# First block's attention taken by pairs of query blocks, with the values as the stationary operand of 256-column matmuls

## The chip, the cores and the metric

The kernel runs on one core of a Trainium2 chip. Its time is the device time of one execution in microseconds; a comparison takes the median of several executions. The profile is one further execution, recorded by the hardware profiler; its times are counted from the start of its span.

## What is computed

Two transformer blocks run one after the other on 2048 tokens of width 1024, all in float32. The change touches only the attention of the first block: 4 heads, queries and keys of 128 + 64 features (the 64 are rotated by position), values of 128, softmax over all 2048 keys with a causal mask by position, then a gate.

```python
def attend(args):
    qn, qr, pq = args
    s = (jnp.einsum('bqhd,bkhd->bhqk', qn, k_nope)
         + jnp.einsum('bqhr,bkr->bhqk', qr, k_rope)).astype(jnp.float32) * scale
    mask = pq[:, None, :, None] >= positions[:, None, None, :]
    p = jax.nn.softmax(jnp.where(mask, s, neg), axis=-1)
    return jnp.einsum('bhqk,bkhd->bqhd', p.astype(v.dtype), v)
...
y_a = mla_branch(...) * jax.nn.silu(gate_a)
```

## The kernel before

The program is written out by hand for each engine; semaphores order the engines against one another. The first block makes keys and values for all tokens, and then goes over four groups of 512 tokens (g = 0 to 3). A group projects its queries and gates, runs the attention of its 4 query blocks of 128 rows, and ends with the output projection (`1out`), which reads the gated attention output from `y_all`, features on the partitions. The second block follows and isn't changed.

Attention goes by units: one query block i and one head h, 16 units in a group, 64 in all. All 2048 keys are taken for every query block. For one unit:

- TensorE makes the scores: 4 tiles of 128 x 512 into four PSUM banks, each with one matmul over 128 features (L1895) and one over the 64 rotated ones (L1899). Neighbouring tiles take the rotated features from the lower and the upper 64 partitions.
- VectorE adds the mask while it moves each tile to the row buffer in `probs` and takes the row's maximum (L1336 to L1343, semaphore `row_max`). `probs` has room for two rows of 2048, which units use in turn.
- ScalarE takes the exponential in place, with the row's sum beside it (L1011, semaphore `probs_made`).
- TensorE turns the row in 16 transposes of 128 x 128 (L1920), four to a bank; ScalarE copies each bank to one of three slots of `prob_t` (L1006); TensorE multiplies the turned probabilities, as stationary operand, with 128 columns of `val` (L1927) and adds up into `o_acc`, which then holds queries on the partitions. `pv_done` counts these groups of four.

On TensorE's queue the scores of unit u stand ahead of the turns and values of unit u - 1. Within a unit the order is: turn 0, turn 1, values 0, turn 2, values 1, turn 3, values 2, values 3 (a turn is 4 transposes, a values step 4 matmuls). After the fourth head VectorE divides by the sums (L1357, L1360, into `o_sb`), TensorE turns the result in 4 transposes (L1906, tile `o_t`), and VectorE multiplies with the gate into `y_all` (L1349).

Six PSUM banks are shared by all tiles in the order of one list: tile number n takes bank n mod 6, and `claim` makes TensorE wait until tile n - 6 has been drained (semaphores `drained`). `tile_ready` counts finished tiles.

Of the kernel before, what the change touches and what calls it, by code (L numbers as in the profile page):

```python
# [7 lines left out]
S = 2048  # L8
P = 128
KC = D // P  # L10
TB = 512
# [51 lines left out]

def mla_units(g):
    return [(BG * g + b, h) for b in range(BG) for h in range(H1)]


def mla_tiles(g):

    units = mla_units(g)  # L70
    for u in range(len(units) + 2):
        if u < len(units):
            yield from [("score", *units[u], c) for c in range(S // TB)]
        if 2 <= u and units[u - 2][1] == H1 - 1:
            yield ("o_t", units[u - 2][0])
        if 1 <= u <= len(units):
            yield from [("prob_t", *units[u - 1], c) for c in range(S // TB)]
# [324 lines left out]
def program(nc, A, out_t):  # L402
# [10 lines left out]
    with ctx:  # L413
# [27 lines left out]
        k_rope = alloc(one, "k_rope", [P, S])  # L441
# [4 lines left out]
        cos = alloc(one, "cos", [P, TB])  # L446
        sin = alloc(one, "sin", [P, TB])
# [4 lines left out]
        mask = alloc(one, "mask", [P, S], bf16)  # L452
# [37 lines left out]
        two.close()  # L490
        mask_i = probs[:, S:S + KC * P].bitcast(i32)
# [96 lines left out]
        o_scaled = sem("o_scaled")  # L588
# [81 lines left out]
        def prev_unit(units, u, g, back):  # L670
            return units[u - back] if u >= back else mla_units(g - 1)[u - back]
# [240 lines left out]
        def _(act):  # L912
# [61 lines left out]
            for g in range(G):  # L974
# [23 lines left out]
                for u in range(len(units) + 1):  # L998
                    if u > 0:
                        i, h = units[u - 1]  # L1000
                        for c in range(S // TB):
                            m = (H1 * BG * g + u - 1) * (S // TB) + c
                            wait_tile(act, "prob_t", i, h, c)
                            if m >= PT_SLOTS:
                                act.wait_ge(pv_done, m - PT_SLOTS + 1)
                            drains(A_(prob_t[:, m % PT_SLOTS, :], bank("prob_t", i, h, c)[:], ACT.Copy), "prob_t", i, h, c)  # L1006
                    if u < len(units):
                        n = H1 * BG * g + u
# [218 lines left out]
        def _(dve):  # L1227
# [45 lines left out]
            for g in range(G):  # L1273
# [3 lines left out]
                step(dve, V.tensor_tensor(k_rope[:, g * TB:(g + 1) * TB], tmp[:, 0, :], tmp[:, 1, :], ALU.add))  # L1277
# [8 lines left out]
            def mask_of(i):  # L1286

                step(dve, V.tensor_scalar(mask[:], pos_k[:], pos_q[:, i:i + 1], MASKED, ALU.is_gt, ALU.mult))

            for g in range(G):  # L1290
# [35 lines left out]
                for u in range(len(units) + 2):  # L1326
                    if u < len(units):
                        i, h = units[u]
                        n = H1 * BG * g + u
                        if h == 0:  # L1330
                            mask_of(i)
                        if n >= 2:
                            wait_tile(dve, "prob_t", *prev_unit(units, u, g, 2), S // TB - 1)
                        for c in range(S // TB):
                            wait_tile(dve, "score", i, h, c)
                            drains(V.tensor_tensor_reduce(out=probs[:, (n % 2) * S + c * TB:(n % 2) * S + (c + 1) * TB],  # L1336
                                                          in0=bank("score", i, h, c)[:], in1=mask[:, c * TB:(c + 1) * TB],
                                                          scale=1.0, scalar=-HUGE, op0=ALU.add, op1=ALU.max,
                                                          accum_out=stat[:, c:c + 1]), "score", i, h, c)
                        for c in range(S // TB):  # L1340
                            wait_drained(dve, "score", i, h, c)
                        step(dve, V.reduce_max(stat[:, 4:5], stat[:, 0:4], AX.X))
                        V.tensor_scalar(stat[:, 8 + n % 2:9 + n % 2], stat[:, 4:5], -QK_DIM ** -0.5, None,  # L1343
                                        ALU.mult).then_inc(row_max, 1)
                    if 2 <= u and units[u - 2][1] == H1 - 1:
# [6 lines left out]
                    if 1 <= u <= len(units) and units[u - 1][1] == H1 - 1:  # L1352
                        i = units[u - 1][0]
# [939 lines left out]
```

## Time and profile before

| | |
|---|---|
| median of 3 executions | 3866.52 us (3864.78 to 3866.83) |
| profiled execution: its time, its span | 3869.51 us, 3867.7 us |
| TensorE busy | 3532.2 us, 91% of the span |
| VectorE, ScalarE, GpSimd busy | 1794.3, 1443.8 and 414.1 us |
| granted TensorE clock, mean | 0.963 of full speed |

The profile lists a float32 matmul as two instructions, since the engine passes over the moving operand twice; a transpose is one. So four matmuls stand as x8 in its rows, and four transposes as x4. A row's own length includes the time in which its last result drains, which overlaps with the next row; what a piece of work costs the engine is the distance from its start to the next row's start. The span contains some 1.8 us less than the time, since launching and ending lie outside it.

### The profile page before, as it was taken

The numbers are of one execution on the slowest core, as the hardware profiler recorded it, in microseconds if no ns is written. First come the engines' busy times: TensorE is split into PE (matmuls) and PEld (weight loads), VectorE is DVE, ScalarE is ACT, GpSimd is POOL, SyncE is SP. The second block draws the span as 40 slices with busy tenths as digits, with TensorE's granted clock in tenths as the row PEclk, the third lists the DMA queues.
The fourth block names the chain that finished last, engine by engine and source line by source line (L and its number), as shares of the span: only waits on it lengthen the run. The fifth ranks groups of instructions, "written<-read, shape, count | busy, mean of one in ns | idle before, by whom it ended". The sixth has DMA issues, their size and how long they took to land.

```text
span 3867.7 us, 40758 instructions
## 1 busy us (share of the span) xinstructions
PE 3532.2 (91%) x15056; PEld 1965.5 (51%) x15056; DVE 1794.3 (46%) x4223; ACT 1443.8 (37%) x2445; POOL 414.1 (11%) x445
## 2 busy tenths in 40 slices
PE   8999999999999999999988989799797898787887
PEld 3445644564466446644555445554445643444653
DVE  3413222331232223223664477825778625879652
ACT  1213312331233113312332355524666515666551
POOL 0001011001200210011111201111011111010100
PEclk9999999999999999989989999899899998998999
DMA  4130013002300230042103211031110031110002
GB/s 172 57 95 23 1 57 117 17 1 65 116 10 1 71 97 1 1 141 82 60 20 100 72 54 47 1 109 66 50 52 1 23 103 53 41 57 1 1 4 85
DMA packets 71893, 205.67 MB, mean 53 GB/s; under 512 B 6376, under 2 KB 7952, under 8 KB 71440
## 3 DMA queue, kind: packets, MB, share of 16 engines
q1 hardware_dynamic: 63360, 187.32, 15.0%
q10 hardware_dynamic: 8336, 15.74, 1.1%
q8 instruction: 121, 1.98, 0.2%
q14 instruction: 76, 0.62, 0.1%
HBM read 185.46 MB, written 17.58 MB: 52 GB/s over the span
## 4 chain that ended last, share of the span: by engine, by line
PE 74%; DVE 11%; ACT 8%; issue 6%; SPq 0%; DMA 0%; POOL 0%; ACTq 0%; DVEq 0%; POOLq 0%
PE bank L1794 38%; PE o_acc L1927 6%; PE bank L1895 6%; PE bank L1899 3%; PE bank L2138 3%; PE bank L2023 3%; PE bank L1920 2%; PE bank L2150 2%; PE o_acc L2164 2%; PE bank L2055 2%; ACT prob_t L1066 2%; ACT pt_last L1066 1%; DVE tmp L1506 1%; ACT prob_t L1006 1%; PE bank L2004 1%
## 5 line engine op out<-in xcount | busy, mean ns | idle before, releaser
L1794 PE MATMUL bank<-group_even,weights 128*128 128x512 f32 x1376 | 603.1, 596 | 17.0 <-DMA weights<-in_w_in_kv 11.7
L1794 PE MATMUL bank<-group_odd,weights 128*128 128x512 f32 x1376 | 607.0, 599 | 6.2 <-ACT tmp L1052 6.2
L1794 PE MATMUL bank<-y_all,weights 128*128 128x512 f32 x1024 | 443.2, 595 | 10.5 <-DVE y_all L1758 6.3
L1794 PEld LDWEIGHTS bank<-group_even,weights 128*128 128x128 f32 x1376 | 261.5, 192 | 337.9 <-issue 337.8
L1794 PEld LDWEIGHTS bank<-group_odd,weights 128*128 128x128 f32 x1376 | 262.5, 193 | 331.2 <-issue 330.9
L1336 DVE CUSTOM_DVE_ANT_0 probs<-bank,mask 128x512 f32<-128x512 f32 x256 | 161.6, 687 | 417.7 <-PE bank L1899 417.7
L1794 PEld LDWEIGHTS bank<-y_all,weights 128*128 128x128 f32 x1024 | 194.5, 191 | 254.4 <-issue 247.1
L1006 ACT ACTIVATE prob_t<-bank 128x512 f32<-128x512 f32 x256 | 145.9, 596 | 430.2 <-PE bank L1920 430.2
L1927 PE MATMUL o_acc<-val,prob_t 128*128 128x128 f32 x2048 | 270.3, 280 | 16.0 <-ACT prob_t L1006 16.0
L1927 PEld LDWEIGHTS o_acc<-val,prob_t 128*128 128x128 f32 x2048 | 247.3, 191 | 31.2 <-ACT prob_t L1006 31.2
L1895 PE MATMUL bank<-k_nope,q_nope 128*128 128x512 f32 x512 | 230.7, 593 | 0.0
L2138 PE MATMUL bank<-kh,qa 64*128 64x512 f32 (+3 forms) x816 | 172.0, 498 | 28.1 <-DVE mx L1716 15.4
L1193 ACT ACTIVATE prob_t<-bank 128x512 f32<-128x512 f32 (+3 forms) x240 | 116.7, 534 | 146.7 <-PE bank L2150 146.4
L2164 PE MATMUL o_acc<-prob_t,v 128*64 128x128 f32 x1680 | 148.0, 284 | 12.2 <-ACT prob_t L1193 8.5
L2164 PEld LDWEIGHTS o_acc<-prob_t,v 128*64 128x64 f32 x1680 | 120.0, 140 | 58.6 <-issue 41.4
L1920 PE MATMUL bank<-ident,probs 128*128 128x128 f32 x1024 | 146.1, 275 | 3.3 <-ACT probs L1011 3.3
L1895 PEld LDWEIGHTS bank<-k_nope,q_nope 128*128 128x128 f32 x512 | 92.7, 190 | 96.8 <-issue 96.8
L1011 ACT ACTIVATE probs<-probs,stat 128x2048 f32<-128x2048 f32 x64 | 127.5, 1993 | 36.8 <-DVE stat L1343 36.8
L1920 PEld LDWEIGHTS bank<-ident,probs 128*128 128x128 f32 x1024 | 115.6, 141 | 40.4 <-issue 36.4
L1899 PE MATMUL bank<-k_rope,q_rope 64*128 64x512 f32 x512 | 127.2, 615 | 0.0
L2150 PE MATMUL bank<-ident,probs 128*128 128x128 f32 x624 | 90.3, 288 | 38.9 <-ACT probs L1202 30.2
L1258 DVE TENSOR_TENSOR tmp<-bank,cos 128x512 f32<-128x512 f32 x12 | 8.3, 692 | 252.7 <-PE bank L1794 249.8
(377 smaller groups left out, 5017.9 us busy)
## 6 DMA issues: line engine op xcount, KB each, us to landing
weights<-in_w_in SPq DMA_DIRECT2D x101, 512.0 KB, 3.6
weights<-in_w_in_q SPq DMA_DIRECT2D x64, 512.0 KB, 3.5
weights<-in_w_out SPq DMA_DIRECT2D x64, 512.0 KB, 3.6
weights<-in_w_i SPq DMA_DIRECT2D x20, 512.0 KB, 3.5
group_even<-in_x_t SPq DMA_DIRECT2D x8, 1024.0 KB, 7.9
group_odd<-in_x_t SPq DMA_DIRECT2D x8, 1024.0 KB, 8.9
group_even<-x_t SPq DMA_DIRECT2D x8, 1024.0 KB, 8.0
group_odd<-x_t SPq DMA_DIRECT2D x8, 1024.0 KB, 7.4
```

Of the source, the lines that this page charges most:

```text
L1006: drains(A_(prob_t[:, m % PT_SLOTS, :], bank("prob_t", i, h, c)[:], ACT.Copy), "prob_t", i, h, c)
L1011: A_(p, p, ACT.Exp, scale=QK_DIM ** -0.5, bias=stat[:, 8 + n % 2:9 + n % 2], accum_out=stat[:, 16 + n % 8:17 + n % 8]).then_inc(probs_made, 1)
L1193: drains(A_(prob_slots[2 * (m % 2) + e][:, 0:wide_], bank("p2_t", i, 2 * p + e, c)[:, 0:wide_], ACT.Copy), "p2_t", i, 2 * p + e, c)
L1336: drains(V.tensor_tensor_reduce(out=probs[:, (n % 2) * S + c * TB:(n % 2) * S + (c + 1) * TB], in0=bank("score", i, h, c)[:], in1=mask[:, ...
L1794: ins = M(bank(*name)[:], ring[n % SLOTS][:, k * P:(k + 1) * P], rhs[:, k, :], start=(k == 0), stop=(k == chunks - 1))
L1895: M(bank("score", i, h, c)[:], q_nope[:, h, b * P:(b + 1) * P], k_nope[:, h, c * TB:(c + 1) * TB], start=True, stop=False)
L1899: M(bank("score", i, h, c)[:], q_rope[half, h, b * P:(b + 1) * P], k_rope[half, c * TB:(c + 1) * TB], start=False, stop=True).then_inc(til ...
L1920: ins = nc.tensor.transpose(bank(*name)[:, k * P:(k + 1) * P], probs[:, col:col + P], ident[:])
L1927: ins = M(o_acc[i % 2][:, h * P:(h + 1) * P], prob_t[:, m % PT_SLOTS, k * P:(k + 1) * P], val[:, c * BG + k, h * P:(h + 1) * P], start=(c ...
L2138: ins = M(bank("s2", i, 2 * p + e, c)[:, at:at + end - first], qa[rows, p, (i % BG) * P:(i % BG + 1) * P], kh[rows, a, p, first:end], star ...
L2150: ins = nc.tensor.transpose(bank("p2_t", i, h, c)[:, (k % BG) * P:(k % BG + 1) * P], probs_of(g, u, e)[:, k * P:(k + 1) * P], ident[:])
L2164: ins = M(o_acc[i % 2][e * DH2:(e + 1) * DH2, p * P:(p + 1) * P], v2[:, k, h * DH2:(h + 1) * DH2], prob_slots[2 * (m % 2) + e][:, (k % BG) ...
```

## The change

A unit is now a pair of neighbouring query blocks (e = 0, 1) and one head: 8 units in a group, 32 in all, each with two half units. The order of the steps is written once, in `mla_steps`, and all engines follow it. The scores of the next unit's first half stand ahead of a unit's turns, those of its second half ahead of the last two values steps. A turn now takes 4 transposes of each of the two blocks; ScalarE copies the two banks into one buffer of 1024 columns so that the two blocks' 128 columns stand side by side for each key block. A values step holds 128 x 128 of `val` stationary and moves 256 columns, 128 of each query block; `o_acc` then has the features on the partitions and needs no turning. What is turned instead is a tile of reciprocal row sums (`share1_t`), once for two heads of a pair; VectorE multiplies it with the gate, and the product with `o_acc` into `y_all`.

There are three row buffers in turn: the two in `probs`, and `lat`, which is free during attention. The turned probabilities have two buffers: two slots of `prob_t`, and the former `cos` and `sin`, now one tensor `turns`. `k_rope` now keeps its upper and lower half for different keys, not twice the same; the mask has a copy for each half.

```diff
+
+
 def mla_units(g):
-    return [(BG * g + b, h) for b in range(BG) for h in range(H1)]
+
+    return [(BG * g + b, h) for b in range(0, BG, 2) for h in range(H1)]
+
+
+def mla_steps(g):
+
+    units = mla_units(g)
+
+    def scores(u, e):
+        return [("score", u, e), ("exp", u, e)] if u < len(units) else []
+
+    yield from scores(0, 0) + scores(0, 1)
+    for u, (i, h) in enumerate(units):
+        first, second = scores(u + 1, 0), scores(u + 1, 1)
+        yield from first[:1]
+        yield from [("turn", u, c) for c in range(2)]
+        yield from first[1:]
+        yield ("value", u, 0)
+        if h % 2 == 0 and u > 0:
+            yield from [("share", u - 1), ("blend", u - 1)]
+        for c in range(2, TILES_1):
+            yield ("turn", u, c)
+            if c < TILES_1 - 1:
+                yield ("value", u, c - 1)
+        yield from second
+        if h % 2 == 1:
+            yield ("sums", u)
+        yield from [("value", u, c) for c in range(TILES_1 - 2, TILES_1)]
+    yield from [("share", u), ("blend", u)]
 
 
 def mla_tiles(g):
 
...
+    for st in mla_steps(g):
+        i, h = units[st[1]]
+        if st[0] == "score":
+            yield from [("score", i + st[2], h, c) for c in range(TILES_1)]
+        elif st[0] == "turn":
+            yield from [("prob_t", i + e, h, st[2]) for e in range(2)]
+        elif st[0] == "share":
+            yield ("share1_t", i, h // 2)
```

Buffers:

```diff
-        k_rope = alloc(one, "k_rope", [P, S])
+        k_rope = alloc(one, "k_rope", [P, S // 2])
...
-        cos = alloc(one, "cos", [P, TB])
-        sin = alloc(one, "sin", [P, TB])
+        turns = alloc(one, "turns", [P, 2, TB])
+        cos, sin = turns[:, 0, :], turns[:, 1, :]
...
-        mask = alloc(one, "mask", [P, S], bf16)
+        mask = alloc(one, "mask", [P, 2, S], bf16)
...
+        probs_1 = probs[:, 0:S], probs[:, S:2 * S], lat[:, :, :].rearrange("p j t -> p (j t)")
+        turned_1 = [a.rearrange("p e t -> p (e t)") for a in (prob_t[:, 0:2, :], turns[:, :, :])]
```

ScalarE:

```diff
-                for u in range(len(units) + 1):
-                    if u > 0:
-                        i, h = units[u - 1]
-                        for c in range(S // TB):
-                            m = (H1 * BG * g + u - 1) * (S // TB) + c
-                            wait_tile(act, "prob_t", i, h, c)
-                            if m >= PT_SLOTS:
-                                act.wait_ge(pv_done, m - PT_SLOTS + 1)
-                            drains(A_(prob_t[:, m % PT_SLOTS, :], bank("prob_t", i, h, c)[:], ACT.Copy), "prob_t", i, h, c)
...
+                for st in mla_steps(g):
+                    kind, u = st[:2]
+                    i, h = units[u]
+                    if kind == "turn":
+                        c = st[2]
+                        m = (len(units) * g + u) * TILES_1 + c
+                        to = turned_1[m % 2].rearrange("p (k e q) -> p k e q", k=BG, e=2)
+                        for e in range(2):
+                            wait_tile(act, "prob_t", i + e, h, c)
+                            if m >= 2 and e == 0:
+                                act.wait_ge(pv_done, m - 1)
+                            drains(A_(to[:, :, e, :], bank("prob_t", i + e, h, c)[:].rearrange("p (k q) -> p k q", k=BG), ACT.Copy),
+                                   "prob_t", i + e, h, c)
+                    elif kind == "exp":
+                        e = st[2]
+                        n = half_units_before(g, u, e)
                         act.wait_ge(row_max, n + 1)
-                        p = probs[:, (n % 2) * S:(n % 2 + 1) * S]
-                        A_(p, p, ACT.Exp, scale=QK_DIM ** -0.5, bias=stat[:, 8 + n % 2:9 + n % 2],
-                           accum_out=stat[:, 16 + n % 8:17 + n % 8]).then_inc(probs_made, 1)
+                        p = probs_1[n % 3]
+                        A_(p, p, ACT.Exp, scale=QK_DIM ** -0.5, bias=stat[:, 8 + n % 3:9 + n % 3],
+                           accum_out=stat[:, 16 + 2 * h + e:17 + 2 * h + e]).then_inc(probs_made, 1)
```

VectorE (the parts that aren't the same work under new names):

```diff
+                            before, q = units[(2 * u + e - 3) // 2]
+                            wait_tile(dve, "prob_t", before + (e + 1) % 2, q, TILES_1 - 1)
...
-                    if 2 <= u and units[u - 2][1] == H1 - 1:
-                        i = units[u - 2][0]
-                        b = i % BG
-                        wait_tile(dve, "o_t", i)
-                        drains(V.tensor_tensor(y_of(g)[:, 0:4, b * P:(b + 1) * P],
-                                               bank("o_t", i)[:].rearrange("p (j t) -> p j t", j=4),
-                                               gate[:, :, b * P:(b + 1) * P], ALU.mult), "o_t", i)
...
-                        i = units[u - 1][0]
-                        dve.wait_ge(pv_done, (i + 1) * H1 * (S // TB))
...
                         step(dve, V.reciprocal(stat[:, 32:36], stat[:, at:at + 4]))
-                        if i > 0:
-                            wait_tile(dve, "o_t", i - 1)
-                        V.tensor_tensor(o_sb[:].rearrange("p (h d) -> p h d", h=H1),
-                                        o_acc[i % 2][:].rearrange("p (h d) -> p h d", h=H1),
-                                        stat[:, 32:36].unsqueeze(2).broadcast_to([P, H1, P]), ALU.mult).then_inc(o_scaled, 1)
...
+                        if u > 1:
+                            before, q = units[u - 2]
+                            wait_tile(dve, "share1_t", before, q // 2)
+                        V.tensor_copy(tmp[:, :, :].rearrange("p a t -> p (a t)")[:, 0:TB].rearrange("p (k q) -> p k q", k=4),
+                                      stat[:, 32:36].unsqueeze(2).broadcast_to([P, 4, P])).then_inc(shares1_made, 1)
+                    elif kind == "blend":
+                        first, at = h - 1, (i % BG) * P
+                        wait_tile(dve, "share1_t", i, h // 2)
+                        share = o_sb[:].rearrange("p (h t) -> p h t", h=2)
+                        drains(V.tensor_tensor(share, bank("share1_t", i, h // 2)[:].rearrange("p (h t) -> p h t", h=2),
+                                               gate[:, first:first + 2, at:at + 2 * P], ALU.mult), "share1_t", i, h // 2)
+                        wait_drained(dve, "share1_t", i, h // 2)
+                        dve.wait_ge(pv_done, (len(units) * g + u + 1) * TILES_1)
+                        V.tensor_tensor(y_of(g)[:, first:first + 2, at:at + 2 * P],
+                                        o_acc[h // 2][:].rearrange("p (h t) -> p h t", h=2), share, ALU.mult).then_inc(y1_made, 1)
```

TensorE:

```diff
+                    elif kind == "turn":
+                        c = st[2]
+                        for e in range(2):
+                            n = half_units_before(g, u, e)
+                            if c == 0:
+                                pe.wait_ge(probs_made, n + 1)
+                            name = ("prob_t", i + e, h, c)
...
-                            wait_drained(pe, "prob_t", i, h, c)
-                            m = n * (S // TB) + c
-                            for k in range(BG):
-                                ins = M(o_acc[i % 2][:, h * P:(h + 1) * P], prob_t[:, m % PT_SLOTS, k * P:(k + 1) * P],
-                                        val[:, c * BG + k, h * P:(h + 1) * P],
-                                        start=(c == 0 and k == 0), stop=(c == S // TB - 1 and k == BG - 1))
-                            ins.then_inc(pv_done, 1)
...
-                        transposes(0)
-                        for c in range(1, S // TB):
-                            transposes(c)
-                            values(c - 1)
-                        values(S // TB - 1)
...
+                    elif kind == "value":
+                        c = st[2]
+                        m = (len(units) * g + u) * TILES_1 + c
+                        if h % 2 == 0 and c == 0 and blends_before(g, u) >= 2:
+                            pe.wait_ge(y1_made, blends_before(g, u) - 1)
+                        for e in range(2):
+                            wait_drained(pe, "prob_t", i + e, h, c)
+                        for k in range(BG):
+                            ins = M(o_acc[h // 2][:, (h % 2) * 2 * P:(h % 2 + 1) * 2 * P], val[:, c * BG + k, h * P:(h + 1) * P],
+                                    turned_1[m % 2][:, 2 * k * P:2 * (k + 1) * P],
+                                    start=(h % 2 == 0 and c == 0 and k == 0), stop=(c == TILES_1 - 1 and k == BG - 1),
+                                    skip_group_check=True)
+                        ins.then_inc(pv_done, 1)
+                    elif kind == "share":
+                        pe.wait_ge(shares1_made, blends_before(g, u) + 1)
+                        claim("share1_t", i, h // 2)
+                        for p in range(4):
+                            ins = nc.tensor.transpose(bank("share1_t", i, h // 2)[:, p * P:(p + 1) * P],
+                                                      tmp[:, 0, p * P:(p + 1) * P], ident[:])
+                        ins.then_inc(tile_ready, 1)
```

TensorE's queue before, from the first group's second unit on: the scores of a unit (bank<-k_nope,q_nope and bank<-k_rope,q_rope), then the previous unit's turns (bank<-ident,probs) and values (o_acc<-val,prob_t).

```order
L1895 MATMUL bank<-k_nope,q_nope 128x512 x4
L1899 MATMUL bank<-k_rope,q_rope 128x512 x4
L1920 MATMUL bank<-ident,probs 128x128 x8
L1927 MATMUL o_acc<-val,prob_t 128x128 x4
L1920 MATMUL bank<-ident,probs 128x128 x4
L1927 MATMUL o_acc<-val,prob_t 128x128 x4
L1920 MATMUL bank<-ident,probs 128x128 x4
L1927 MATMUL o_acc<-val,prob_t 128x128 x8
```

The same queue and place in the changed kernel, for one pair:

```order
L1949 MATMUL bank<-k_nope,q_nope 128x512 x4
L1953 MATMUL bank<-k_rope,q_rope 128x512 x4
L1965 MATMUL bank<-ident,probs 128x128 x16
L1975 MATMUL o_acc<-prob_t,val 128x256 x4
L1965 MATMUL bank<-ident,probs 128x128 x8
L1975 MATMUL o_acc<-turns,val 128x256 x4
L1965 MATMUL bank<-ident,probs 128x128 x8
L1949 MATMUL bank<-k_nope,q_nope 128x512 x4
L1953 MATMUL bank<-k_rope,q_rope 128x512 x4
L1975 MATMUL o_acc<-prob_t,val 128x256 x4
L1975 MATMUL o_acc<-turns,val 128x256 x4
```

Two units of before have 32 values matmuls of 128 columns in six runs; a pair has 16 of 256 columns in three runs, with 16 transposes ahead of the first run where there were 8, and other work between a turn and its values at every other place.

ScalarE's queue in the changed kernel, within that pair (row buffers appear as probs or lat): copies of turns 0 and 1, the exponential of the next unit's first half, and copies of turns 2 and 3.

```order
L1049 ACTIVATE prob_t<-bank 128x4x128 x2
L1049 ACTIVATE turns<-bank 128x4x128 x2
L1056 ACTIVATE lat,stat<-lat,stat 128x2048
L1049 ACTIVATE prob_t<-bank 128x4x128 x2
```

Before, all four copies of a unit stood in a row and one exponential behind them; now an exponential stands between the second and the third turn's copies.

## Rows read from the trace of the kernel before

**Rows 1.** The page: busy time by engine, and the chain that ended last.

```profile
PE 3532.2 (91%) x15056; PEld 1965.5 (51%) x15056; DVE 1794.3 (46%) x4223; ACT 1443.8 (37%) x2445; POOL 414.1 (11%) x445
...
PE 74%; DVE 11%; ACT 8%; issue 6%; SPq 0%; DMA 0%; POOL 0%; ACTq 0%; DVEq 0%; POOLq 0%
```

**Rows 2.** Windows, first score to first `1out` of a group; first and fourth.

```profile
312.09:499.69 187.60, 180.74 (x1042) 121.59 (x1040) 57.07 (x178) 69.55 (x97) 0.00 (x0) 1.00 0.00 1
...
1451.01:1638.61 187.60, 180.74 (x1041) 121.59 (x1040) 57.06 (x178) 68.27 (x96) 0.00 (x0) 1.00 0.00 1
```

The columns are the stretch, its length, busy time (and count) of PE, PEld, DVE, ACT and POOL, the granted clock, the DMA share and GB/s.

**Rows 3.** Timeline of PE, a unit and the next: start, length, work.

```profile
397.85 3.60 PE L1895 MATMUL bank<-k_nope,q_nope 128*128 128x512 f32 x8
401.38 1.99 PE L1899 MATMUL bank<-k_rope,q_rope 64*128 64x512 f32 x8
403.30 1.09 PE L1920 MATMUL bank<-ident,probs 128*128 128x128 f32 x8
404.64 1.16 PE L1927 MATMUL o_acc<-val,prob_t 128*128 128x128 f32 x8 [0.25 <-ACT prob_t L1006]
405.63 0.60 PE L1920 MATMUL bank<-ident,probs 128*128 128x128 f32 x4
406.07 1.06 PE L1927 MATMUL o_acc<-val,prob_t 128*128 128x128 f32 x8
406.96 0.60 PE L1920 MATMUL bank<-ident,probs 128*128 128x128 f32 x4
407.40 2.01 PE L1927 MATMUL o_acc<-val,prob_t 128*128 128x128 f32 x16
409.24 3.60 PE L1895 MATMUL bank<-k_nope,q_nope 128*128 128x512 f32 x8
...
414.69 0.65 PE L1906 MATMUL bank<-ident,o_sb 128*128 128x128 f32 x4
415.18 1.04 PE L1920 MATMUL bank<-ident,probs 128*128 128x128 f32 x8
```

**Rows 4.** Waits of PE, 312 to 1639 us: in total, times, longest.

```profile
PE o_acc L1927 <- ACT prob_t L1006: 16.0, 64, 0.3
```

**Rows 5.** Timeline of PE in the second block: 64 rows, 256 columns.

```profile
2063.90 1.16 PE L2138 MATMUL bank<-kh,qa 64*128 64x256 f32 x8
2064.99 0.32 PE L2164 MATMUL o_acc<-prob_t,v 128*64 128x128 f32 x1
```

**Rows 6.** Timeline of ACT in the unit of rows 3.

```profile
403.99 1.09 ACT L1006 ACTIVATE prob_t<-bank 128x512 f32<-128x512 f32 x2 [5.21 <-PE bank L1920]
```

**Rows 7.** Groups by form, 300 to 500 us.

```profile
L1927 PEld LDWEIGHTS o_acc<-val,prob_t 128*128 128x128 f32 x512 | 61.8, 191 | 7.8 <-ACT prob_t L1006 7.8
L1006 ACT ACTIVATE prob_t<-bank 128x512 f32<-128x512 f32 x64 | 36.5, 596 | 107.6 <-PE bank L1920 107.6
L1360 DVE TENSOR_TENSOR o_sb<-o_acc,stat 128x512 f32<-128x512 f32 x4 | 2.8, 691 | 0.1
L1349 DVE TENSOR_TENSOR y_all<-bank,gate 128x512 f32<-128x512 f32 x4 | 2.7, 683 | 0.8 <-PE bank L1906 0.8
```

**Rows 8.** Timeline of all engines, end of the first group's attention.

```profile
483.94 1.09 PE L1920 MATMUL bank<-ident,probs 128*128 128x128 f32 x8
...
486.15 0.15 DVE L1343 TENSOR_SCALAR stat<-stat 128x1 f32<-128x1 f32 x1
...
488.74 1.99 ACT L1011 ACTIVATE probs<-probs,stat 128x2048 f32<-128x2048 f32 x1
490.88 1.09 PE L1920 MATMUL bank<-ident,probs 128*128 128x128 f32 x8 [0.82 <-ACT probs L1011]
...
494.98 2.01 PE L1927 MATMUL o_acc<-val,prob_t 128*128 128x128 f32 x16
...
497.99 0.66 PE L1906 MATMUL bank<-ident,o_sb 128*128 128x128 f32 x4 [1.00 <-DVE o_sb L1360]
498.69 0.69 DVE L1349 TENSOR_TENSOR y_all<-bank,gate 128x512 f32<-128x512 f32 x1 [0.75 <-PE bank L1906]
499.69 6.64 PE L1794 MATMUL bank<-y_all,weights 128*128 128x512 f32 x11 [1.04 <-issue]
```

More of the change, by code:

```diff
@@ L1276, in _ @@
                 rotate("krope", g)
-                step(dve, V.tensor_tensor(k_rope[:, g * TB:(g + 1) * TB], tmp[:, 0, :], tmp[:, 1, :], ALU.add))
+                rows = slice((g % 2) * ROPE, (g % 2 + 1) * ROPE)
+                step(dve, V.tensor_tensor(k_rope[rows, (g // 2) * TB:(g // 2 + 1) * TB], tmp[rows, 0, :], tmp[rows, 1, :], ALU.add))
                 wait_drained(dve, "kv_sq", g)
@@ new lines, in _ @@
+                pe.wait_ge(q_rotated, g + 1)
+                if g == 0:
+                    for hh in range(H1):
+                        wait_drained(pe, "k_nope", G - 1, hh)
+                for st in mla_steps(g):
+                    kind, u = st[:2]
+                    i, h = units[u]
+                    if kind == "score":
+                        e = st[2]
+                        cols = slice((i % BG + e) * P, (i % BG + e + 1) * P)
+                        for c in range(TILES_1):
+                            claim("score", i + e, h, c)
+                            M(bank("score", i + e, h, c)[:], q_nope[:, h, cols], k_nope[:, h, c * TB:(c + 1) * TB],
@@ L1896, in _ @@
                               start=True, stop=False)
-                        for c in range(S // TB):
+                        for c in range(TILES_1):
                             half = slice((c % 2) * ROPE, (c % 2 + 1) * ROPE)
-                            M(bank("score", i, h, c)[:], q_rope[half, h, b * P:(b + 1) * P],
-                              k_rope[half, c * TB:(c + 1) * TB], start=False, stop=True).then_inc(tile_ready, 1)
-                    if 2 <= u and units[u - 2][1] == H1 - 1:
-                        i = units[u - 2][0]
-                        pe.wait_ge(o_scaled, i + 1)
-                        claim("o_t", i)
-                        for j in range(4):
-                            ins = nc.tensor.transpose(bank("o_t", i)[:, j * P:(j + 1) * P], o_sb[:, j * P:(j + 1) * P], ident[:])
-                        ins.then_inc(tile_ready, 1)
@@ L1908, in _ @@
-                    if 1 <= u <= len(units):
-                        i, h = units[u - 1]
-                        n = H1 * BG * g + u - 1
-                        pe.wait_ge(probs_made, n + 1)
-                        if h == 0 and i >= 2:
-                            pe.wait_ge(o_scaled, i - 1)
-                        def transposes(c):
-                            name = ("prob_t", i, h, c)
+                            M(bank("score", i + e, h, c)[:], q_rope[half, h, cols],
+                              k_rope[half, (c // 2) * TB:(c // 2 + 1) * TB], start=False, stop=True).then_inc(tile_ready, 1)
+                    elif kind == "turn":
+                        c = st[2]
+                        for e in range(2):
+                            n = half_units_before(g, u, e)
+                            if c == 0:
+                                pe.wait_ge(probs_made, n + 1)
+                            name = ("prob_t", i + e, h, c)
```

84 lines of the change are left out of this document (34 added, 50 removed).

## Prediction

> **What bounds the kernel now.** The page comes first: TensorE is busy 91% of the span and carries 74% of the chain that ended last [rows 1]. Then the windows, one for each group's attention. Each is 187.60 us long, first score to first `1out`; the two in between agree, so the four make 750.4 us. In each of them TensorE is busy for 180.74 us, VectorE for 57.07 and ScalarE for 69.55, at a granted clock of 1.00 and with next to no DMA [rows 2]. No engine but TensorE is near its limit there, and a microsecond off its queue in this stage is a microsecond off the end. "Busy" hides something, though: a matmul's row includes its drain. The timeline by starts shows what a unit costs [rows 3]. Scores take from 397.85 to 403.30, 5.45 us. Turns and values take from 403.30 to 409.24, 5.94 us. Together 11.39 us.
>
> In those 5.94 us the steady prices are: four transposes 0.44 (405.63 to 406.07), so 0.11 each; eight passes of values 0.89 (406.07 to 406.96), so 0.111 each. Sixteen transposes and 32 passes make 1.76 + 3.56 = 5.32 us. The other 0.62 us is waiting and restarting: the first values stand 1.34 us behind the first of eight transposes, which need 0.88, so 0.46 is lost: 0.05 is the start of transposes behind scores (the row of L1906 shows 0.49 for four there, 0.05 over steady), and 0.41 the wait for the copy, of which the waits show 0.25 each time [rows 3, 4]. The first eight passes behind it take 0.99 instead of 0.89, the last sixteen 1.84 instead of 1.78.
>
> **The wait that goes.** Values 0 need one copy, and it begins 0.69 us behind the first transpose (403.30 to 403.99, [rows 3, 6]); there are only eight transposes to cover it. In the changed order 16 transposes stand there, 1.76 + 0.05 = 1.81 us. But values 0 now need two copies. Two take 1.09 us [rows 6], so they end 0.69 + 1.09 = 1.78 us behind the first transpose, and the values could start at 1.83. The wait shrinks from 0.41 to 0.02, once for a pair where it was twice. I keep the restart costs, 0.10 at the first values of a pair and 0.06 at the last, since every first instruction behind a semaphore is fresh: with the 0.05 and 0.02 that is 0.23 us for a pair, against 1.24 before.
>
> **Passes of 256 columns.** The trace has none of 128 rows. A 128-column pass costs 0.111; one of 512 costs 0.43 (four matmuls, eight passes, 397.85 to 401.38, less 0.09 for the switch). On the line between them 256 columns cost 0.217. The second block has 256-column passes on 64 rows, two side by side: eight take 1.09 us, four pass times [rows 5]; the same with 512 columns takes 1.92 (401.38 to 403.30, [rows 3]), so 256 columns more cost 0.83 / 4 = 0.21. The bounds are 0.208 from this and 0.222, twice a 128-column pass; I take 0.217. A pair has 32 such passes, 6.94 us, for 64 of 0.111, 7.10. The longer moving operand by itself gains only 0.16 us for a pair, 5 us in all. The load of the stationary values, 191 ns in its row and already finished within passes that follow at 0.111 [rows 7], has more cover than before.
>
> **Sum.** A pair: scores 10.90, transposes 32 x 0.11 = 3.52, values 6.94, restarts and wait 0.23: 21.59 us. Two units before: 22.78. The gain is 1.19 us for a pair, 38.1 us for 32. The turning of shares costs what that of outputs did: four transposes at 16 places each, 0.49 in its row. At a group's end, the last values of before are followed by division, transposes, gate: from 494.98 + 1.84 to 499.69, 2.87 us [rows 8]. Now the transposes follow at once; VectorE starts 0.70 behind them, does two operations of 0.69 with 0.05 between, and `1out` begins 0.31 later (498.69 + 0.69 to 499.69): 2.44 us. That is 0.43 less, 1.7 for four groups. The last exponential of a group has no scores ahead of its turn. The row maximum is there 2.36 us behind the scores, the exponential takes 2.14 to its reader (488.74 to 490.88), 4.55 with a hop [rows 8]; two values steps cover 3.52. It waits 1.03, where 0.99 were waited before (488.05 + 1.84 to 490.88). No change. Sum: 39.8 us. The profiled execution took 3869.51 and would take 3829.7; it stands 3 us over the median of 3866.52, from which I get **3827 us**.
>
> **Edits at nothing.** Within a group the same 4.55 us of row maximum and exponential are covered by 3.52 of values and 5.45 of scores, 8.97: 4.4 us of slack. The third row buffer is needed for that; a half unit's row is overwritten three half units on, and its last turn stands just ahead of those scores on TensorE's queue. On ScalarE's queue the copies of turn 2 stand behind an exponential. It starts 2.4 us behind the first transpose, or when four copies are done, 0.69 + 4 x 0.53 = 2.8; it ends at 4.9. Turn 2 ends at about 4.6, so its copies are done by 6.0. Who waits for them is the third bank of the next scores, claimed at about 8.0, then values 2 behind those scores. Slack 2 us. VectorE gets one more operation for every two heads (about 0.69, 16 times) with 57 of 187 us busy. Mask copies, `k_rope` halves, gate by pairs: no more elements than before. SP's loads for `1out` go by ring slots free before attention begins.
>
> **Rivals.** *Restarts stay.* Every values step now waits for two semaphores, and copies of one bank could be late at each: nothing in the rows excludes 0.1 to 0.3 us at some of the five switches of a pair. With the old 0.41 kept once for a pair the gain falls by 0.39 x 32 = 12.5: 3840 us. For it speaks that the covered margin is 0.02 only; against it, the second and third values of a unit show no wait [rows 3].
>
> *Passes cost by number, not by columns.* If 256 columns cost what 128 do, 0.111, a pair saves 3.39 us more, 108 in all: about 3719 us. Against it stands the 0.43 of 512 columns, 3.9 times the 128-column pass. The Trainium skill (TensorE: Matmul & The Clock Gate, Back-to-back issue gap) gives 81 ns for 128 and 131 ns for 512 columns in a stream of loads and matmuls, which would make doubling nearly free (256 columns at 1.2 times the 128, and about 3741 us, as an estimate from that page). By that rule, this case's trace disagrees, with 0.111 and 0.43 us.
>
> *Copies become dearer.* They now write four pieces of 128 with gaps. A copy behind another costs 0.49; each 0.1 more delays the first values by 0.2, 6.4 us in all. At half the rate (0.47 more, from the 0.60 and 1.99 us of 512 and 2048 columns) a pair loses 0.94: 3857 us, no change that can be told. If besides each piece started anew (about 0.13 x 3), a pair loses 1.72: 39.8 - 55 = -15 us, **3882 us, slower**. It decides at a copy 0.62 us dearer. Against it: VectorE's gate multiply writes just such four pieces in 683 ns, the contiguous division 691 [rows 7].
>
> **How the numbers follow.** The forecast 3816 to 3838: 0.76. Its ends: 0.208 a pass (0.29 less for a pair, 9 us) and 2 us of the restarts gone give 3816; 0.222 a pass (5 us) and 0.2 us of further restarts for a pair (6 us) 3838. Restarts stay, 3838 to 3850: 0.13. Below 3816, by a cheap pass or fewer restarts than any row shows: 0.04. Copies dearer: within 0.2% 0.04, slower 0.03. The range 3816 to 3843 holds the forecast and half of the first rival. A measurement of this kernel can tell 0.2%, 7.7 us: faster 0.93, the same 0.04, slower 0.03.
>
> **What would show it.** After: each group's window 177 to 178 us; scores still 5.45; 256-column passes of 128 rows 0.217 apart (the last sixteen of a pair in about 3.5 us); first values 1.83 behind the first of 16 transposes, with a wait on `prob_t` of a few hundredths; copies still near 596 ns. Wrong if a new wait on `probs` or `y_all` stands inside a group, if copies take over 0.7 us, or if time outside the four windows moves.

## The result, and the profile after

The changed kernel takes 3823.74 us (median, 3822.57 to 3828.17) where the kernel before took 3865.65 beside it: a ratio of 0.989, with an interval of 0.9878 to 0.9901. That is 41.9 us less; 39.8 us less and a time of 3827 us were forecast.

The page of the changed kernel has TensorE 92% busy, and the chain is as much TensorE's as in [rows 1].

```profile
PE 3506.6 (92%) x14032; PEld 1922.5 (50%) x14032; DVE 1800.8 (47%) x4239; ACT 1434.6 (38%) x2445; POOL 414.2 (11%) x445
...
PE 75%; DVE 11%; ACT 7%; issue 6%; SPq 0%; DMA 0%; POOL 0%; ACTq 0%; DVEq 0%; POOLq 0%
```

The windows of the four groups, first score to first `1out`, in the columns of [rows 2]:

```profile
311.83:489.05 177.22, 175.33 (x786) 111.32 (x784) 58.78 (x182) 67.39 (x97) 0.00 (x0) 1.00 0.00 1
...
1418.03:1595.26 177.23, 175.34 (x785) 111.32 (x783) 58.78 (x182) 66.09 (x96) 0.00 (x0) 1.00 0.00 1
```

All four are 177.2 us long instead of 187.60: 4 x 10.38 = 41.5 us, and that accounts for the 41.9 us between the medians. TensorE's busy time in a window fell by only 5.4 us; the other 5 were idle time that is gone. The two profiled executions differ by more, 46.9 us in span. Of the 5.4 us outside the windows, 1.7 follow a stretch at half clock behind the first group of before (last section). Another 3.6 lie between the last `1out` and the end, in work that wasn't changed: 2229.1 us in one profile and 2225.5 in the other, and 2223.2 to 2229.1 over all nine profiles of this text. So that difference is within what this stretch varies by from kernel to kernel; what varies it wasn't tried.

The timeline of TensorE in the changed kernel, one pair of the first group (to hold against [rows 3]; this pair has the four transposes of a share tile, L1984):

```profile
371.67 0.66 PE L1965 MATMUL bank<-ident,probs 128*128 128x128 f32 x4
...
373.04 0.60 PE L1965 MATMUL bank<-ident,lat 128*128 128x128 f32 x4
373.59 1.97 PE L1975 MATMUL o_acc<-prob_t,val 128*128 128x256 f32 x8
375.39 0.60 PE L1984 MATMUL bank<-ident,tmp 128*128 128x128 f32 x4
...
376.70 1.89 PE L1975 MATMUL o_acc<-turns,val 128*128 128x256 f32 x8
378.43 0.60 PE L1965 MATMUL bank<-ident,probs 128*128 128x128 f32 x4
...
379.31 3.60 PE L1949 MATMUL bank<-k_nope,q_nope 128*128 128x512 f32 x8
382.84 1.99 PE L1953 MATMUL bank<-k_rope,q_rope 64*128 64x512 f32 x8
384.75 1.99 PE L1975 MATMUL o_acc<-prob_t,val 128*128 128x256 f32 x8
386.58 1.89 PE L1975 MATMUL o_acc<-turns,val 128*128 128x256 f32 x8
388.31 3.60 PE L1949 MATMUL bank<-k_nope,q_nope 128*128 128x512 f32 x8
391.84 1.99 PE L1953 MATMUL bank<-k_rope,q_rope 64*128 64x512 f32 x8
393.76 0.44 PE L1965 MATMUL bank<-ident,probs 128*128 128x128 f32 x2
```

From the first transpose to the next pair's first transpose it is 393.76 - 371.67 = 22.09 us, less 0.44 for the share tile 21.65; 21.59 was forecast, and two units took 22.78. A pass is one of the two instructions in which a float32 matmul stands in the rows; the rows show that there are two, and nothing of what the engine does in each. Eight passes of 256 columns take 1.73 us (376.70 to 378.43), 0.216 each. The first values stand 1.92 us behind the first transpose. TensorE's waits of the changed kernel over the whole stage no longer have `prob_t` [rows 4] in them:

```profile
PE bank L1847 <- DVE y_all L1414: 6.0, 4, 1.5
PE bank L1965 <- ACT probs L1056: 1.2, 3, 0.4
PE bank L1965 <- ACT lat L1056: 0.4, 1, 0.4
```

The first is the end of a group. The others are the last turn of a group, which waits for its exponential. (A row's wait counts only idle time, so the 0.12 us by which the first values are later than 16 transposes at their steady price, 1.80 us, don't appear in it.) Copies kept their price with four separated pieces, 598 and 602 ns against 596 [rows 7]:

```profile
L1049 ACT ACTIVATE prob_t<-bank 128x512 f32<-128x512 f32 x32 | 17.5, 598 | 35.0 <-PE bank L1965 34.8
L1049 ACT ACTIVATE turns<-bank 128x512 f32<-128x512 f32 x32 | 17.4, 602 | 11.1 <-PE bank L1965 11.1
```

### The profile page after: what moved, and what is told of

It reads as the page before. It is cut to its first block, busy times and chain, and to the rows that moved or that the text cites. A ratio compares the mean times of both kernels' runs of the same rounds, so it can differ in the third digit from the quotient of the medians.

```text
span 3820.8 us, 38713 instructions
## 1 busy us (share of the span) xinstructions
PE 3506.6 (92%) x14032; PEld 1922.5 (50%) x14032; DVE 1800.8 (47%) x4239; ACT 1434.6 (38%) x2445; POOL 414.2 (11%) x445
## 3 DMA queue, kind: packets, MB, share of 16 engines
q8 instruction: 114, 1.87, 0.2%
## 4 chain that ended last, share of the span: by engine, by line
PE 75%; DVE 11%; ACT 7%; issue 6%; SPq 0%; DMA 0%; POOL 0%; ACTq 0%; DVEq 0%; POOLq 0%
PE bank L1847 38%; PE bank L1949 6%; PE o_acc L1975 6%; PE bank L1953 3%; PE bank L1965 3%; PE bank L2187 3%; PE bank L2072 3%; PE bank L2199 2%; PE o_acc L2213 2%; PE bank L2104 2%; ACT prob_t L1111 2%; ACT pt_last L1111 1%; DVE tmp L1559 1%; PE bank L2053 1%; DVE rstd L1507 1%
## 5 line engine op out<-in xcount | busy, mean ns | idle before, releaser
L1385 DVE CUSTOM_DVE_ANT_0 probs<-bank,mask 128x512 f32<-128x512 f32 x172 | 108.5, 687 | 261.9 <-PE bank L1953 261.9
L1056 ACT ACTIVATE probs<-probs,stat 128x2048 f32<-128x2048 f32 x43 | 86.5, 2012 | 171.2 <-DVE stat L1395 171.2
L1303 DVE TENSOR_TENSOR tmp<-bank,turns 128x512 f32<-128x512 f32 x12 | 8.3, 691 | 252.7 <-PE bank L1847 249.8
L1975 PE MATMUL o_acc<-prob_t,val 128*128 128x256 f32 x512 | 126.3, 389 | 0.0
L2199 PE MATMUL bank<-ident,probs 128*128 128x128 f32 x624 | 89.6, 287 | 39.4 <-ACT probs L1247 30.1
L1049 ACT ACTIVATE prob_t<-bank 128x512 f32<-128x512 f32 x128 | 70.0, 600 | 140.1 <-PE bank L1965 139.2
L2187 PEld LDWEIGHTS bank<-kh,qa 64*128 64x128 f32 x816 | 80.3, 195 | 82.9 <-issue 36.7
L1975 PE MATMUL o_acc<-turns,val 128*128 128x256 f32 x512 | 121.0, 379 | 0.0
L1247 ACT ACTIVATE probs<-probs,stat 128x128 f32<-128x128 f32 (+15 forms) x86 | 91.3, 1063 | 78.7 <-DVE stat L1782 78.6
```

The costliest lines, as they stand in the source:

```text
L1385: drains(V.tensor_tensor_reduce(out=probs_1[n % 3][:, c * TB:(c + 1) * TB], in0=bank("score", i + e, h, c)[:], in1=mask[:, e, c * TB:(c + ...
L1975: ins = M(o_acc[h // 2][:, (h % 2) * 2 * P:(h % 2 + 1) * 2 * P], val[:, c * BG + k, h * P:(h + 1) * P], turned_1[m % 2][:, 2 * k * P:2 * ( ...
L2187: ins = M(bank("s2", i, 2 * p + e, c)[:, at:at + end - first], qa[rows, p, (i % BG) * P:(i % BG + 1) * P], kh[rows, a, p, first:end], star ...
L2199: ins = nc.tensor.transpose(bank("p2_t", i, h, c)[:, (k % BG) * P:(k % BG + 1) * P], probs_of(g, u, e)[:, k * P:(k + 1) * P], ident[:])
```

## The experiments

The change does two things at once: it puts more transposes between a turn and its values, and it lets a values pass move 256 columns. The theory was that the first gives nearly all, the rival that the second does. The two are taken apart from either side. Window lengths are the sharpest measure, since the four groups of a run agree within 0.02 us (in one run 0.14); times are given beside them. Each ratio is to the kernel before as measured beside that run, at 3866.91 us for four of the seven and at 3864.78 for "More cover", "One semaphore" and the last one.

**256 columns undone.** Each values matmul is cut into two of 128 columns on the same stationary block.

```diff
                         for k in range(BG):
-                            ins = M(o_acc[h // 2][:, (h % 2) * 2 * P:(h % 2 + 1) * 2 * P], val[:, c * BG + k, h * P:(h + 1) * P],
-                                    turned_1[m % 2][:, 2 * k * P:2 * (k + 1) * P],
...
+                            for e in range(2):
+                                at = ((h % 2) * 2 + e) * P
+                                ins = M(o_acc[h // 2][:, at:at + P], val[:, c * BG + k, h * P:(h + 1) * P],
+                                        turned_1[m % 2][:, (2 * k + e) * P:(2 * k + e + 1) * P],
...
```

> The changed kernel, with each values matmul of 256 moving columns cut into two of 128 (one query block each) on the same stationary 128 x 128 of val; order, buffers and waits as changed. Theory (the gain comes from covered waits, the longer moving operand gives next to nothing): a pair has 64 passes of 0.111 us instead of 32 of 0.216, 0.2 us more; each group's window 177.2 + 1.6 = 178.8 us, the time 6 us over the changed kernel, about 3830 us. Rival (256 columns are what gains, since stationary loads are halved): most of the gain goes, windows of 184 us or more, time 3850 us or more.

Measured: 3831.4 us (ratio 0.9908, 0.989 to 0.9925). The windows of this kernel:

```profile
311.82:490.80 178.98, 177.21 (x1041) 120.76 (x1039) 58.78 (x182) 67.38 (x97) 0.00 (x0) 1.00 0.00 1
...
1423.30:1602.28 178.98, 177.21 (x1041) 120.73 (x1039) 58.78 (x182) 66.09 (x96) 0.00 (x0) 1.00 0.00 1
```

The windows are 1.76 us longer than in the changed kernel, 7.0 in all (6 expected), with twice the loads of stationary values in the values passes. Of 41.5 us, the longer moving operand is worth 7.

**Only the order, in the kernel before.** One query block a unit, two row buffers, 128 columns, three slots; only turn 2 goes ahead of values 0.

```diff
                         transposes(0)
-                        for c in range(1, S // TB):
+                        transposes(1)
+                        for c in range(2, S // TB):
                             transposes(c)
-                            values(c - 1)
+                            values(c - 2)
+                        values(S // TB - 2)
                         values(S // TB - 1)
```

> The kernel before, units of one query block and 128 columns, with only the order on TensorE and its tile list unchanged in kind: turn 2 is issued ahead of values 0 (turns 0, 1, 2, values 0, turn 3, values 1, 2, 3). Twelve transposes, 1.37 us, then cover the copy that ends 1.29 us behind the first. Theory (the wait for the copy was 0.41 us for a unit and its restart 0.10): windows of 187.6 - 16 x 0.41 to 0.51 = 179.4 to 181.0 us, time 3833 to 3840 us, most of the change's gain without any pair. Rival (the wait returns at values 1 or at a bank, or pairs were needed for it): windows of 185 us or more, time over 3855 us.

Measured: 3833.71 us (ratio 0.9915, 0.990 to 0.9931). Its windows, and its timeline of TensorE in a unit:

```profile
312.76:491.62 178.86, 176.82 (x1042) 120.72 (x1040) 57.08 (x178) 67.83 (x97) 0.00 (x0) 1.00 0.00 1
...
1428.82:1607.67 178.85, 176.81 (x1042) 120.68 (x1040) 57.06 (x178) 66.55 (x96) 0.00 (x0) 1.00 0.00 1
```

```profile
400.51 1.53 PE L1920 MATMUL bank<-ident,probs 128*128 128x128 f32 x12
401.87 1.14 PE L1927 MATMUL o_acc<-val,prob_t 128*128 128x128 f32 x8
402.85 0.60 PE L1920 MATMUL bank<-ident,probs 128*128 128x128 f32 x4
403.28 2.84 PE L1927 MATMUL o_acc<-val,prob_t 128*128 128x128 f32 x24
405.96 3.60 PE L1895 MATMUL bank<-k_nope,q_nope 128*128 128x512 f32 x8
...
480.47 2.84 PE L1927 MATMUL o_acc<-val,prob_t 128*128 128x128 f32 x24
483.31 1.53 PE L1920 MATMUL bank<-ident,probs 128*128 128x128 f32 x12
```

The values follow the twelve transposes without a gap (401.87 - 400.51 = 1.36 us), and the windows lose 8.74 us, 35.0 in all, somewhat more than expected (8.2 at most). The turns and values of a unit take 5.45 us (400.51 to 405.96) instead of 5.94: 0.49 less, as expected, 7.8 for 16 units. Most of the rest, 0.8 us, has another source. The group's last turn waits for its exponential, and before, that exponential stood on ScalarE's queue behind the four copies of the unit ahead. The kernel before, TensorE's and ScalarE's timelines (its turn began at 490.88, [rows 8]):

```profile
488.05 2.01 PE L1927 MATMUL o_acc<-val,prob_t 128*128 128x128 f32 x16
...
488.25 0.60 ACT L1006 ACTIVATE prob_t<-bank 128x512 f32<-128x512 f32 x1 [0.73 <-PE bank L1920]
488.74 1.99 ACT L1011 ACTIVATE probs<-probs,stat 128x2048 f32<-128x2048 f32 x1
```

With turn 2 ahead of values 0 the copies end sooner, and the last turn starts 0.16 us late (483.31 - 480.47 = 2.84 us for 24 passes of 2.68 us) where it started 0.99 late. So 84% of the window gain of the change is to be had by moving one turn, without pairs, third buffer or turned outputs; of the time it is 33.2 us. That 35.0 + 7.0 = 42 come near the 41.5 of the change is no proof by itself, since the 35.0 contain 3.3 us at the four last exponentials, where the change gains otherwise (below).

**A spare copy.** Is there slack left at the first values of a pair?

```diff
+                            if c == 0 and e == 0:
+                                A_(std[:], bank("prob_t", i, h, 0)[:], ACT.Copy)
                             drains(A_(to[:, :, e, :], ...
```

> The changed kernel, with one spare copy of the first turned bank of every pair into an unused tile, ahead of the real one on ScalarE. Theory (nothing is left of cover at the first values: 16 transposes 1.81 us, two copies end at 1.78 us): the whole 0.49 us of a copy lands on the path of every pair, windows of 177.2 + 8 x 0.49 = 181.1 us, 15.7 us more in all, about 3839 us. Rival (the first values have slack on ScalarE, which is busy 67 of 177 us): windows within 0.5 us of 177.2, time within 2 us of the changed kernel.

Measured: 3840.12 us (ratio 0.9932, 0.9917 to 0.9948), windows of 180.76 us, 3.54 more. TensorE's waits of this run:

```profile
PE o_acc L1977 <- ACT prob_t L1051: 12.5, 28, 0.4
```

There is no slack: the wait returned, 28 times rather than 32, with 0.45 us. The missing four are the last pair of each group, where the second block's exponential comes late anyway and spreads the transposes out. 7 x 0.5 = 3.5 us is the lengthening.

**Less cover.** Values 0 go behind turn 0, ahead of turn 1.

```diff
-        yield from [("turn", u, c) for c in range(2)]
-        yield from first[1:]
-        yield ("value", u, 0)
+        yield ("turn", u, 0)
+        yield ("value", u, 0)
+        yield ("turn", u, 1)
+        yield from first[1:]
```

> The changed kernel, with values 0 of a pair issued behind turn 0, ahead of turn 1, so that 8 transposes stand ahead of them where there are 16 now. Theory (the copies end at 1.78 us whatever TensorE does meanwhile): the 0.88 us of turn 1 no longer cover anything, windows of 177.2 + 8 x 0.88 = 184.2 us, 28 us more, about 3852 us. Rival (the cover matters little and 256 columns carry the gain): windows under 180 us, time under 3835 us.

Measured: 3856.28 us (ratio 0.997, 0.996 to 0.9981), windows of 185.18 us, 7.96 more.

```profile
328.09 1.09 PE L1966 MATMUL bank<-ident,probs 128*128 128x128 f32 x8
330.01 1.97 PE L1976 MATMUL o_acc<-prob_t,val 128*128 128x256 f32 x8 [0.83 <-ACT prob_t L1050]
331.81 1.91 PE L1966 MATMUL bank<-ident,probs 128*128 128x128 f32 x16
333.68 1.97 PE L1976 MATMUL o_acc<-turns,val 128*128 128x256 f32 x8
```

The values start at 330.01 - 328.09 = 1.92 us, as in the changed kernel, whether 8 or 16 transposes stand ahead: the copies set that moment. The 0.88 us of turn 1 are paid again, and so are another 0.12 ahead of values 1 (333.68 - 331.81 = 1.87 us for 16 transposes, 0.12 over 1.75) and 0.07 in their first pass, since values 1 now stand as close behind their copies as values 0 do. With pairs, buffers and 256 columns kept and only the cover taken, 32 of 41.5 us are gone.

**More cover.** Values 3 of a pair move behind turn 1 of the next, except at the last pair, whose exponential they cover.

```diff
         yield from [("turn", u, c) for c in range(2)]
+        if 0 < u < len(units) - 1:
+            yield ("value", u - 1, TILES_1 - 1)
...
-        yield from [("value", u, c) for c in range(TILES_1 - 2, TILES_1)]
+        yield ("value", u, TILES_1 - 2)
+        if u >= len(units) - 2:
+            yield ("value", u, TILES_1 - 1)
```

> The changed kernel, with values 3 of a pair moved behind turn 1 of the next pair (for six of the eight pairs of a group), so that they stand between turns 0 and 1 and values 0. Theory (the changed kernel still loses about 0.2 us at the first values of each pair, 0.12 until they start and 0.08 in their first pass): that goes six times in a group, windows of 177.2 - 1.2 = 176.0 us, time 4.7 us under the changed kernel, about 3819 us. Rival (the restart only moves to another place, or the copies of turn 1, which now wait for these values, come late for values 1): windows of 177 us or more.

Measured: 3821.27 us (ratio 0.9887, 0.9872 to 0.9901), windows of 176.06 us, 1.16 less:

```profile
392.97 1.97 PE L1969 MATMUL bank<-ident,probs 128*128 128x128 f32 x16
394.77 1.89 PE L1979 MATMUL o_acc<-turns,val 128*128 128x256 f32 x8
396.50 1.89 PE L1979 MATMUL o_acc<-prob_t,val 128*128 128x256 f32 x8
398.22 1.04 PE L1969 MATMUL bank<-ident,probs 128*128 128x128 f32 x8
```

From the transposes on, everything follows at its steady price: 1.80 us for 16 transposes, 1.73 for each eight passes. The windows are shorter than in both kernels, by 4.65 us in all against the changed one; the times of the two were taken at different hours and overlap (3819.55 to 3822.87 here, 3822.57 to 3828.17 there), so that only the windows show it.

**One semaphore.** The wait for the first of two copies goes ahead of the last four transposes.

```diff
                             claim(*name)
+                            if (c, e) == (1, 1):
+                                wait_drained(pe, "prob_t", i, h, 0)
...
-                        for e in range(2):
+                        for e in range(1 if c == 0 else 0, 2):
```

> The changed kernel, with the wait for the copy of turn 0's first block put ahead of the last four transposes of turn 1, so that the first values wait for one semaphore where they waited for two. Theory (of the 0.12 us lost ahead of the first values some 0.08 is the second semaphore, taken by an instruction of its own, and only some 0.03 the copy): windows of 177.2 - 8 x 0.08 = 176.6 us, 2 to 3 us less in all. Rival (the copy itself is late, and the number of semaphores costs nothing): windows unchanged at 177.2 us.

Measured: 3824.24 us (ratio 0.9894, 0.9879 to 0.9909), windows of 176.84 us in the first group and 176.97 to 176.98 in the others.

```profile
329.85 2.06 PE L1967 MATMUL bank<-ident,probs 128*128 128x128 f32 x16
331.75 1.93 PE L1977 MATMUL o_acc<-prob_t,val 128*128 128x256 f32 x8
333.51 1.04 PE L1967 MATMUL bank<-ident,probs 128*128 128x128 f32 x8
```

The windows are 0.25 us shorter in three groups and 0.38 in one, where the theory had 0.64 and the rival nothing: neither came true, and the time (3823.74 us for the changed kernel) shows no difference. The first eight passes take 1.76 instead of 1.80 us, but the values still begin 1.90 us behind the first transpose, where it was 1.92, and the row of the transposes, which now has two semaphores at one place, grew from 1.96 to 2.06. Moving the wait mostly moved its price. How the 0.12 us divides between the copy and the second semaphore stays open.

## Why the prediction was right, step by step

*The wait that goes.* Right, and the main term. It is shown from both sides: adding cover alone to the kernel before gives 35 us, 31 of them inside the units, and taking it from the changed one costs 32. For waits and restarts the forecast was 1.24 - 0.23 = 1.01 us for a pair, 32 us. The rival *Restarts stay*, by which the old 0.41 us would be kept once for a pair, is out: 0.12 us is left ahead of the first values, and no other values of the pair begin late.

*Start of the first values.* Put at 1.83 us, measured 1.92. The pair came out at 21.65 instead of 21.59 us, 2 us in all.

*Restarts.* 0.16 us a pair was kept for them, and 0.17 came out, but not for the reason given, that every first instruction behind a semaphore is fresh. Values 1 also begin behind a semaphore and take the steady 1.73 us (376.70 to 378.43). The restarts stand at the first values, which TensorE reaches with a wait (1.80, 0.07 over), and at the values right behind the scores' matmuls over 64 features (384.75 to 386.58, 1.83, 0.10 over). The size was luck.

*Passes of 256 columns.* 0.217 us by the line between 128 and 512 columns, 0.216 measured. The gain was given as 5 us and the run with 128 columns lost 7. The rival *Passes cost by number* is out, and so is the nearly free doubling priced beside it: a pass of 256 columns costs 1.95 times one of 128.

*A group's end.* Mis-sized to the good side. From the last values' end to `1out` I had 2.44 us; it is 489.05 - 486.94 = 2.11, as `1out` starts 0.06 us behind the last product, not 0.31. And the last turn loses only 0.54 us, where the prediction had 1.03. Its chain of row maximum and exponential was sized right: the second block's transposes begin 4.54 us behind the scores (472.23 to 476.77), for 4.55. But the four transposes of the pair's first block need only the first exponential and go ahead while the second finishes, which the prediction overlooked. It also misread the 0.99 us of before, which were set by the copies ahead of the exponential and not by this chain, so that "No change" rested on two numbers that were alike by chance. The timeline of TensorE in the changed kernel:

```profile
472.23 1.99 PE L1975 MATMUL o_acc<-prob_t,val 128*128 128x256 f32 x8
474.06 1.89 PE L1975 MATMUL o_acc<-turns,val 128*128 128x256 f32 x8
475.79 0.60 PE L1965 MATMUL bank<-ident,lat 128*128 128x128 f32 x4
476.77 0.66 PE L1965 MATMUL bank<-ident,probs 128*128 128x128 f32 x4 [0.39 <-ACT probs L1056]
```

Together that is 0.8 us a group, 3.3 in all, which more than offsets the pair's 2 us. So the forecast's 39.8 us for windows that gained 41.5 is two small misses of opposite sign. As to the hop behind the last product, the trace of before has two instructions on TensorE's queue that only wait for semaphores, of 51 ns each at 499.48 and 499.58, between the product's end at 499.38 and `1out`; the changed kernel has none there. That they are the 0.25 us is a reading of the two traces and wasn't tried.

*Edits at nothing.* Held: TensorE has no wait on a bank, row buffer or `y_all` inside a group. *Copies become dearer*: they didn't (598 and 602 ns), but the price worked out for it did hold, 0.45 to 0.5 us for a spare copy at full length on the path.

*One sign of being wrong did appear.* "If time outside the four windows moves": in the profiled executions it moved by 5.4 us. It doesn't touch the account, since 1.7 us of it are the half clock behind one group and 3.6 lie within what the unchanged second block varies by; between the medians nothing is left over (41.9 for 41.5 us). The sign as written was too strict to tell the one from the other.

## What to carry to other kernels

On an engine that is the bound, read the distance between starts, not the busy share: half a microsecond in each unit of 11.4 was lost at one place, between the transposes and the first product that needs their copy. Count how long the copies take from the first transpose (0.69 us and 0.5 for each), and put that much independent work there; moving one turn was worth five sixths of what the rewrite gained in the windows. A longer moving operand saves only what a pass costs beyond its columns, here 0.006 us of 0.111, so price it from two lengths in the trace before building for it.

## What the hardware did unexpectedly

Behind the idle time at a group's end the clock of TensorE can fall to its lower level. In the kernel before, the windows of 3.5 us that begin with `1out`, first and second group:

```profile
499.70:503.20 3.50, 3.50 (x5) 1.51 (x6) 0.00 (x0) 0.00 (x0) 0.00 (x0) 0.52 0.00 0
880.45:883.90 3.45, 3.45 (x8) 1.59 (x9) 0.00 (x0) 0.00 (x0) 0.00 (x0) 1.00 0.00 0
```

At 0.52 of full speed, close to 1.2 of 2.4 GHz, five passes start where eight do otherwise, and the way to the next group's scores is 193.16 instead of 191.48 us: 1.7 us. It happened after one of four groups in the kernel before, and after all four in the run with the third turn. There each of the three ways to a next group is 193.14 to 193.18 us, some 5 us more than in the kernel before over the four if the last cost the same, which hides part of that order's gain in its time. Ahead of `1out` TensorE idles twice for 1.0 us in these two kernels, with four transposes between. In the changed kernel it idles once for 1.5, and the clock fell in none of its four group ends and none of the 20 of the five experiments that keep this idle time. One run lengthened this on purpose, by two spare VectorE operations:

```diff
                         wait_drained(dve, "share1_t", i, h // 2)
+                        if u == len(units) - 1:
+                            for _ in range(2):
+                                step(dve, V.tensor_tensor(rstd[:], share[:, :, :].rearrange("p h t -> p (h t)"), share[:, :, :].rearrange("p h t -> p (h t)"), ALU.mult))
```

> The changed kernel, with two spare VectorE operations of 0.69 us ahead of the last product of every group, so that TensorE idles about 3 us ahead of the output projection where it idled 1.5. Theory (idle time at a group's end also lets the clock fall, as in the first group of before and in all four of the run with the third turn): windows of 177.2 + 1.5 = 178.7 us, the first passes of the output projection at half clock, and 1.7 us more from a group's end to the next group, 193.2 for 191.5; time 6 + 7 = 13 us over the changed kernel, about 3837 us. Rival (the clock isn't tied to this idle time): 191.5 stays, time about 3830 us.

Measured: 3836.74 us (ratio 0.9926, 0.9909 to 0.9943), windows of 178.67 us as expected, and the first passes of `1out` in its four groups:

```profile
491.92:495.40 3.48, 3.48 (x8) 1.62 (x9) 0.00 (x0) 0.00 (x0) 0.00 (x0) 1.00 0.02 5
862.11:865.60 3.49, 3.49 (x5) 1.53 (x6) 0.00 (x0) 0.00 (x0) 0.00 (x0) 0.59 0.02 5
1233.98:1237.50 3.52, 3.52 (x5) 1.48 (x6) 0.00 (x0) 0.00 (x0) 0.00 (x0) 0.62 0.02 5
1605.87:1609.30 3.43, 3.43 (x5) 1.47 (x6) 0.00 (x0) 0.00 (x0) 0.00 (x0) 0.64 0.02 5
```

With 2.96 us of idle time the clock fell in three groups of four, and behind two of them, where the way to a next group can be read, it took 193.21 us for 191.51. The tie to idle time is shown: nothing else was changed, and 0 of 24 group ends became 3 of 4. What decides in the single case isn't: here one group escapes, and the same idle time of twice 1.0 us brought 1 of 4 in one kernel and 4 of 4 in another. A spare stall there costs itself and often 1.7 us more.
